# The slot table of the experts, built by matmuls of 0/1 rank tiles instead of a scatter through memory

## The reference, cut to what matters

```python
lg = (xf @ w_router_group + b_router_group)          # 4 groups
gi = argmax(lg); p_grp = max(softmax(lg))
le = (xf @ w_router_expert + b_router_expert).reshape(-1, 4, 8)
le_g = sum(le * one_hot(gi, 4)[:, :, None], axis=1)
top_v, top_i = top_k(le_g, 2)
wts = softmax(top_v) * p_grp                          # gate weights
e_idx = gi[:, None] * 8 + top_i                       # two of 32 experts a token
out = sum over the two: wts * (silu(x Wgate_e) * (x Wup_e)) Wdown_e
```

## Time and profile before

| what | us |
|---|---|
| median of 3 runs (1534.4 to 1539.6) | 1537.83 |
| the profiled execution | 1539.11 |
| its span, first to last instruction | 1537.4 |
| PE busy (81% of the span) | 1242.3 |
| DVE busy (34%) | 516.8 |
| POOL busy (18%) | 269.1 |
| ACT busy (13%) | 197.2 |

### The profile page before, as it was taken

The page is one execution under the profiler, slowest core; times in us unless marked ns, Lnnn a source line. Parts: engine busy times, 40 slices in busy tenths (PEclk is TensorE's granted clock), DMA queues, the critical chain, the costliest instruction groups (busy, mean ns, idle before and its releaser), DMA issues.

```text
span 1537.4 us, 14850 instructions
## 1 busy us (share of the span) xinstructions
PE 1242.3 (81%) x5948; PEld 683.2 (44%) x5948; DVE 516.8 (34%) x1014; ACT 197.2 (13%) x319; POOL 269.1 (18%) x580
## 2 busy tenths in 40 slices
PE   5899999998979797989979785877888786878625
PEld 2456556454546464656557472332333332333214
DVE  2412657544752862245531331211112111111044
ACT  1311111101201310231210220000000000000011
POOL 3170388870000000021120002010000010000010
PEclk9899999999998898889989866999899998899856
DMA  9998468765663636352122503999999999999441
GB/s 343 363 364 299 166 216 277 268 225 177 215 222 110 219 110 219 125 150 84 55 69 110 218 31 103 421 421 419 413 413 404 404 394 413 400 412 409 203 137 69
DMA packets 140342, 387.06 MB, mean 252 GB/s; under 512 B 15435, under 2 KB 54757, under 8 KB 112814
## 3 DMA queue, kind: packets, MB, share of 16 engines
q1 hardware_dynamic: 132208, 361.91, 62.4%
q0 software_dynamic: 6784, 18.76, 3.5%
q10 hardware_dynamic: 1280, 5.42, 1.0%
HBM read 385.97 MB, written 23.15 MB: 266 GB/s over the span
## 4 chain that ended last, share of the span: by engine, by line
PE 47%; DMA 26%; DVE 10%; POOL 10%; issue 3%; ACT 2%; SPq 1%; DVEq 0%; POOLq 0%; ACTq 0%
DMA slot<-in_w_exp_up 20%; PE psum L1402 10%; PE psum L1069 9%; PE psum L1102 5%; PE psum L1347 5%; PE psum L998 3%; PE psum L959 2%; DMA slot<-in_w_ada 2%; PE psum L968 2%; POOL mem L529 2%; POOL mem L532 2%; POOL sq L527 2%; POOL sq L530 2%; PE psum L1357 1%; POOL sq L528 1%
## 5 line engine op out<-in xcount | busy, mean ns | idle before, releaser
L1402 PE MATMUL psum<-slot,mem 128*64 128x512 f32 x1024 | 259.8, 667 | 83.6 <-DMA slot<-in_w_exp_up 82.7
L1069 PE MATMUL psum<-hT,slot 128*128 128x320 f32 (+1 forms) x1056 | 309.7, 454 | 19.8 <-DMA slot<-in_w_in 19.8
L1069 PEld LDWEIGHTS psum<-hT,slot 128*128 128x128 f32 (+1 forms) x1056 | 205.8, 198 | 120.5 <-issue 28.7
L1402 PEld LDWEIGHTS psum<-slot,mem 128*64 128x64 f32 x1024 | 86.0, 154 | 255.9 <-issue 170.8
L2110 DVE TENSOR_TENSOR sq<-sq,psum 128x256 f32<-128x256 f32 x16 | 6.8, 422 | 381.7 <-ACT sq L914 381.7
L1426 PE MATMUL psum<-mem,sq 128*64 128x512 f32 x512 | 113.4, 595 | 8.6 <-issue 7.1
L968 PE MATMUL psum<-slot,cT 128*8 128x512 f32 (+1 forms) x768 | 101.9, 639 | 16.9 <-DMA slot<-in_w_ada 16.9
L613 POOL DMA_INDIRECT moe_output<-mem,idx x16 | 15.9, 995 | 485.1 <-ACT mem L918 461.5
L1102 PE MATMUL psum<-mem,slot 128*128 128x320 f32 x256 | 78.5, 467 | 0.0
L1347 PE MATMUL psum<-mem,slot 128*128 128x320 f32 x256 | 72.2, 447 | 5.4 <-DVE mem L1945 5.4
L1426 PEld LDWEIGHTS psum<-mem,sq 128*64 128x64 f32 x512 | 42.0, 137 | 69.8 <-issue 67.9
(11 more groups left out here) (422 smaller groups left out, 1323.4 us busy)
## 6 DMA issues: line engine op xcount, KB each, us to landing
slot<-in_w_ada SPq DMA_DIRECT2D x48, 2048.0 KB, 13.7
slot<-in_w_exp_gate SPq DMA_DIRECT2D x64, 1024.0 KB, 13.4
slot<-in_w_exp_up SPq DMA_DIRECT2D x64, 1024.0 KB, 16.6
mem<-in_w_exp_down SPq DMA_DIRECT2D x32, 2048.0 KB, 18.2
slot<-in_w_in SPq DMA_DIRECT2D x17, 2048.0 KB, 17.3
slot<-in_w_out SPq DMA_DIRECT2D x8, 2048.0 KB, 9.0
mem<-in_w_in SPq DMA_DIRECT2D x2, 2048.0 KB, 17.9
mem<-in_x_prompt ACTq DMA_DIRECT2D x1, 2048.0 KB, 12.0
```

Source lines behind the costliest of these rows:

```text
L1069: last = mm(psum[0:wd, grp % 2, 0:T], w[:, k, q * P:q * P + wd], hT[:, k, :], start=(k == 0), stop=(k == KD - 1))
L1402: last = mm(psum[rows_, 0, :].rearrange("p (w n) -> p w n", w=2), xe[i % 2][:, k, rows_], gate_up[h][:, :, k, :], start=(k == 0), stop=(k ...
```

## The change

The table in memory, its six scatters and its read back go. In their place DVE builds, for each choice c and token tile j, a 0/1 tile `at_rank` (token by 64 ranks: 1 where the token's rank is that rank) and a tile `tok_of` (token by expert, holding the token number plus one where the token chose that expert, else 0; a second copy holds the row number plus one). The product, 64 ranks by 32 columns, summed over the six (c, j) in PSUM, is the slot table: 12 matmuls, six for even and six for odd experts, which land on partitions 0 to 63 and 64 to 127. DVE turns 0 into NOWHERE, subtracts one and casts into `slot_rows`, whose layout becomes two blocks of 16 columns. The numbers of `routed` move: 2 is `at_rank`, 3 is `slot_rows`, 4 the overflow counts, 5 `pos_gather`, 6 `spill`. The gate weights and what depends on them come behind the table. PE waits for `routed` 6 behind the first four `turn_x` instead of ahead of them. POOL's consts shrink from seven small steps to two.

```diff
 gpsimd:
-            pl(g.iota(eTi, pattern=[[1, NPAIR], [CAP * NPAIR, 2]], base=0, channel_multiplier=0))
-            for c in range(2):
-                pl(g.iota(tok_row[:, c, :, 0], pattern=[[P, 3]], base=0, channel_multiplier=1))
-                pl(g.iota(tok_row[:, c, :, 1], pattern=[[P, 3]], base=c * T, channel_multiplier=1))
-            pl(g.memset(slot_rows, NOWHERE), "slot_consts")
+            pl(g.iota(count_i, pattern=[[1, CAP]], base=0, channel_multiplier=0))
+            pl(g.iota(tok_next, pattern=[[P, 3]], base=1, channel_multiplier=1), "slot_consts")
-            pool.dma_start(tok_dram.rearrange("(p i) u -> p (i u)", p=P), slot_rows).then_inc(S("tokens_moved"), 16)
-            pool.wait_ge(S("tokens_moved"), 16)
...
             pool.wait_ge(S("routed"), 3)
-            for c in range(2):
-                for j in range(3):
-                    n = P if j < 2 else TS
-                    pool.indirect_dma_start(tok_dram, bass.IndirectOffsetOnAxis(ap=pos_scatter[0:n, 3 * c + j:3 * c + j + 1], axis=0),
-                                            tok_row[0:n, c, j, :], None, bounds_check=NE * CAP - 1, oob_is_err=False)\
-                        .then_inc(S("tokens_moved"), 16)
-            pool.wait_ge(S("tokens_moved"), 16 * 7)
-            pool.dma_start(slot_rows, tok_dram.rearrange("(p i) u -> p (i u)", p=P)).then_inc(S("tokens_moved"), 16)
-            pool.wait_ge(S("tokens_moved"), 16 * 8)
             pool.wait_ge(S("h2_stored"), 32)
 tensor:
             pe.wait_ge(S("routed"), 2)
+            for h in range(2):
+                for c in range(2):
+                    for j in range(3):
+                        n = P if j < 2 else TS
+                        last = mm(psum[CAP * h:CAP * h + CAP, 3, 128:160], at_rank[0:n, 3 * c + j, :],
+                                  tok_of[0:n, c, j, h].rearrange("p w i -> p (w i)"),
+                                  start=(c == 0 and j == 0), stop=(c == 1 and j == 2))
+            last.then_inc(S("rank"), 1)
+            pe.wait_ge(S("routed"), 4)
             mm(bank(3, 3), ones[:, :], rt[:, 496:499], start=True, stop=True).then_inc(S("rank"), 1)
...
             pe.wait_ge(S("act_rows"), 12)
-            pe.wait_ge(S("routed"), 5)
             for g_ in range(4):
                 turn_x(0, g_, 0)
+            pe.wait_ge(S("routed"), 6)
 vector, behind the one-hots (the same A1, A2 and Mk steps, now first; then):
+            st(v.memset(rk, 0.0))
+            dve.wait_ge(S("slot_consts"), 1)
+            st(v.tensor_copy(count_f, count_i))
+            st(v.tensor_copy(tok_f[:, 0, :], tok_next))
+            st(ts(tok_f[:, 1, :], tok_f[:, 0, :], float(T), None, ADD))
+            for c, A_ in enumerate((A1, A2)):
+                for w in range(2):
+                    st(tt(tok_of[:, c, :, :, w, :], A_.rearrange("p j (i h) -> p j h i", h=2),
+                          bc(tok_f[:, c * w, :].unsqueeze(2).unsqueeze(3), [P, 3, 2, NPAIR]), MUL))
+            dve.wait_ge(S("rank"), 1)
+            st(v.tensor_copy(rk[:, 0:2, :], bank(3, 64).rearrange("p (j e) -> p j e", j=2)))
+            st(v.tensor_copy(rk[0:64, 2, :], bank(3, NE, 64, lo=64)))
+            over, sl_, keep, at = rt[:, 484:490], rt[:, 490:496], rt[:, 500:506], rt[:, 472:478]
+            for c, A_ in enumerate((A1, A2)):
+                st(tt(am, A_, rk, MUL))
+                st(v.tensor_reduce(at[:, 3 * c:3 * c + 3].unsqueeze(2), am, AX.X, ADD))
+            st(tt(at_rank, bc(count_f.unsqueeze(1), [P, 6, CAP]), bc(at.unsqueeze(2), [P, 6, CAP]), ALU.is_equal), "routed")
+            st(ts(over, at, float(CAP), None, ALU.is_ge))
+            st(tt(rt[:, 496:499], over[:, 0:3], over[:, 3:6], ADD))
+            dve.wait_ge(S("rank"), 2)
+            found, row = psum[:, 3, 128:160], rt[:, 432:464]
+            st(ts(row, found, 0.0, float(NOWHERE + 1), ALU.is_equal, MUL))
+            st(tt(row, row, found, ADD))
+            st(ts(row, row, -1.0, None, ADD))
+            st(v.tensor_copy(slot_rows, row), "routed")
+            st(v.memset(rt[:, 471:472], 0.0), "routed")
+            st(ts(keep, over, -1.0, 1.0, MUL, ADD))
+            st(ts(sl_, tok_f.rearrange("p c j -> p (c j)"), -1.0, None, ADD))
+            st(tt(rt[:, 478:484], sl_, keep, MUL))
+            st(v.tensor_copy(pos_gather, rt[:, 478:484]), "routed")
+            dve.wait_ge(S("rt_exp"), 1)
   (here the six gate weight steps; then, as before, ge, A1 *= w1, A2 *= w2, comb (2), wk (2), rank, spill;)
-   (the old steps for eT, ge, Mk, over, pos_scatter, sl_ and pos_gather are gone from behind rank 1)
```

More of the change, by code:

```diff
@@ L262, in build @@
         U32 = mybir.dt.uint32
[L263 to L269, removed]
+        idx_ = sb("idx", [P, 44], U32)
+        pos_gather, spill, tok_next = idx_[:, 0:6], idx_[:, 6:7].bitcast(I32), idx_[:, 8:11].bitcast(I32)
+        slot_rows = idx_[:, 12:44]
         gate_up = [slot[:, 2 * h:2 * h + 2, :].rearrange("p w (k n) -> p w k n", k=KD) for h in range(2)]
@@ L281, in build @@
         tri = flat[:, 18432:18560]
-        eTi = flat[:, 18624:18656].bitcast(I32)
-        eT = tri[:, 0:32]
+        count_i = flat[:, 18592:18656].bitcast(I32)
         wr = flat[:, 18684:18684 + KD * 36].rearrange("p (k e) -> p k e", k=KD)
@@ L288, in build @@
         A1, A2, Mk, rk, ge, am = (sq[:, 0, 96 * i:96 * i + 96].rearrange("p (j e) -> p j e", j=3) for i in range(6))
+        at_rank = sq[:, 1, 0:384].rearrange("p (c r) -> p c r", c=6)
+        tok_of = rows[:, 0:384].rearrange("p (c j h w i) -> p c j h w i", c=2, j=3, h=2, w=2)
+        count_f, tok_f = rows[:, 384:448], rows[:, 448:454].rearrange("p (c j) -> p c j", c=2)
         sg = sq[:, 1, 0:256]
@@ L298, in build @@
         act_ = flat[:, 16320:16320 + 640]
-        tok_dram = nc.dram_tensor("rows_of_slot", [NE * CAP, 2], U32, kind="Internal").ap()
         h2_dram = nc.dram_tensor("moe_input", [T, D], F32, kind="Internal").ap()
@@ L444, in _ @@
             gate, up = (a[f"w_exp_{x}"][0].rearrange("e (k p) n -> e p k n", p=P) for x in ("gate", "up"))
-            sp.wait_ge(S("routed"), 5)
+            sp.wait_ge(S("routed"), 6)
             with sp.If(sp.value_load(spill[0:1, :], min_val=0, max_val=2 * T) > 0):
@@ L919, in _ @@
                  .then_inc(S("y_right"), 1)
-            act.wait_ge(S("routed"), 5)
+            act.wait_ge(S("routed"), 6)
             for j in range(3):
@@ L2043, in _ @@
             st(tt(rt[:, 240:243].unsqueeze(2), v2, v1, SUB), "rt_expo")
+            for g in range(4):
+                for A_, oh_ in ((A1, oh1), (A2, oh2)):
+                    st(tt(A_[:, :, 8 * g:8 * g + 8], oh_, bc(oh4[:, :, g:g + 1], [P, 3, 8]), MUL))
+            st(v.memset(A1[64:P, 2, :], 0.0))
+            st(v.memset(A2[64:P, 2, :], 0.0))
+            st(tt(Mk, A1, A2, ADD), "routed")
+            st(v.memset(rk, 0.0))
[28 more added lines that the diff above has]
+            st(v.tensor_copy(pos_gather, rt[:, 478:484]), "routed")
             dve.wait_ge(S("rt_exp"), 1)
@@ L2092, in _ @@
             st(tt(wk[:, 3:6].unsqueeze(2), w2, keep[:, 3:6].unsqueeze(2), MUL))
-            dve.wait_ge(S("rank"), 2)
+            dve.wait_ge(S("rank"), 3)
             st(v.tensor_reduce(rt[:, 499:500], bank(3, 3), AX.X, ADD))
```

32 lines of the change are left out of this document (2 added, 30 removed).

## The result

The changed kernel took 1526.87 us (median of 4, 1526.31 to 1531.13); the kernel before 1536.59 us (median of 4) beside it. The ratio is 0.994, 95% interval 0.9921 to 0.9959. Run twice more beside the kernel before, the same changed kernel gave 1529.96 us (6 executions; ratio 0.994, 0.9926 to 0.9955) and 1529.13 us (8 executions; 0.9949, 0.9932 to 0.9965). The forecast was 1530.0 us, 7.8 us faster, which is a ratio of 0.9949.

A forecast was written before the change was run, and what follows sets the result against it. The DMA stream of expert weights is full, but the router sets its start. Moving the first gather from 936.33 to 928.5 us, limited by the rows' store, saves 7.8 us: 1537.83 to 1530.0 us, range 1526.0 to 1535.0 us.

The forecast's parts named there:

- The gain is in the twelve microseconds between table and gather, and counts one to one: Between scatter positions and first gather, 12.43 us: gather at 928.5 instead of 936.33 us, 7.8 us gained, all on the path.
- Gate weights, earlier matrices and POOL's early part bring nothing: Ahead of the ranks: Mk some 1.8 us earlier, but rank matmuls queue behind transposes; PE does not wait for POOL.
- From the ranks to the table: DVE and PE from 919.1 us: copies, `at_rank`, twelve calls of 3.6 us, four DVE steps, to 926.0 us (925.1, 929.5).
- The store ends last: At POOL's first gather: store of rows lands at 927.7 us, gather at 928.5 us; the table alone would allow 926.9 us.
- the 0.8 us that the forecast left open: In the store of rows: without scatters beside it, it might land some 0.8 us earlier, giving 8.6 us instead of 7.8.
- Waits added: Behind the table: DVE's later steps end about 930.3 us, first gathered rows transposed from 933.1 us; at least 2.8 us left.
- The transposes in front of the ranks: PE before the ranks: they follow ACT's copies, which the change doesn't touch; end at 917.92 us, `rank` 1 stays at 919.1 us.
- The table as the later one: Rival at the first gather: table ends last, gather at 930.4 us, 5.9 us gained, 1531.9 us; chance 0.17.
- The clock that brings more: Rival at transposes and `hidden` 0: clock stays at 2.4 GHz, with faster store 11.1 us gained, 1526.7 us; chance 0.10.
- The stream that gives it back: Rival in the expert-weight stream: 1% less rate loses 4.7 us, leaving 3.1 us, 1534.7 us; no measurable change, chance 0.11.
- Slower by a late clock: Rival at `hidden` 0 and pair 0's down matmuls: 1.2 GHz all the way, 10.6 us lost, 1548.4 us; chance 0.05.

The follow-up runs named there:

- Twelve scatters: Kernel before with each of the six scatters sent a second time, into a second table nobody reads: 1545.27 us against 1537.89 us, ratio 1.005.
- the third profile: Profile from the third set of the changed kernel, no edit, beside the kernel before: 1529.13 us, ratio 0.9949.
- gate weights late: Kernel before with only the gate-weight steps moved behind `pos_gather`: ratio 0.9987 to the kernel before.
- Table twice: Changed kernel with the twelve matmuls of the table made twice: ratio 0.9976 to the kernel before.
- Fill: Changed kernel with 18 unread matmuls of 512 columns in PE's idle times at the router: ratio 0.9978 to the kernel before.
- both together: Changed kernel with the expert-input store in three parts from SP's queue and 15 unread 512-column matmuls in PE's idle times: 1531.08 us, ratio 0.9956.
- the pad: Changed kernel with 24 small unread matmuls far from the router, twelve behind each of pairs 5 and 9: 1531.5 us, ratio 0.9956.
- the store in three: Changed kernel with the expert-input store sent in three parts from SP's queue, each once its rows are copied: 1528.73 us, ratio 0.9946.
- wide logits: Changed kernel with router columns as weights and all 320 tokens moving, 16 logit calls for 48, then turned: 1519.8 us, ratio 0.9897.

## Why the prediction was right, point by point

- **The gain is in the twelve microseconds between table and gather, and counts one to one.** Right. Forecast 7.8 us; 7.8 us at the first load of pair 1 (72.61 to 64.81), 8.1 us between the means. Twelve scatters show the one to one from the other side. The time itself, 1526.87 us, was 3.1 us under the forecast, which is within the spread: the two later medians are 1529.96 and 1529.13 us.
- **Gate weights, earlier matrices and POOL's early part bring nothing.** Right; DVE's idle time in front of the ranks was 4.27 us after, with the `tok_of` steps already out of it, and the edit alone moved no scatter. Without POOL's store at 784 us PE waits 5.43 us for DVE ahead of its matmuls of 320 columns, as before.
- **From the ranks to the table.** Reckoned 6.9 us from 919.1 to 926.0 us; measured 6.92 us (920.17 to 927.09). `at_rank` 0.56 us as its row of before; the twelve calls 3.72 us where I took 3.6, in the third profile 2.80 us. That term came out by two errors that cancel. I let the clock fall at 922.9 us, in the middle of the calls; it fell at about 921.4 us (the granted clock is 1.00 from 921 to 921.4 us and 0.50 from 921.8 us on), so all twelve ran at the low level. And a call at the low level took 3.72 / 12 = 0.31 us, not 0.42 us. In the third profile the clock fell 1.6 us into the calls (1.00 to 928 us, 0.83 from 928 to 929 us, then 0.50). As the store ended last, none of this is in the gain.
- **The store ends last.** Right, and the size of the slack too: reckoned 928.5 - 926.9 = 1.6 us, measured 1.46 us, in the third profile 2.5 us. The last part of the store took 8.39 us against 8.5 us before, so the scatters had hardly slowed it, and the 0.8 us that the forecast left open for this did not come. The estimate from the Trainium skill (DMA: Bandwidth & Descriptors, Anatomy of one DMA) was 8.0 us from the first issue to landing; the trace has 928.55 - 919.73 = 8.82 us, so the row was the better guide, and the page's fit stands for another queue. That the fixed part is mostly the receipt of the last write no run here shows; the 1.90 us of the 16 KB read back bear out its size alone.
- **Waits added.** Right: `spill` was ready at 931.48 us, the first gathered rows were turned from 933.94 us. The margin was 2.5 us where I had 2.8.
- **What I had not in the sum.** The transposes in front of the ranks, which I had as untouched, took 6.25 instead of 5.35 us in the profiled execution. That made the gather only 53.91 - 46.86 = 7.05 us earlier there, and with equal transposes (third profile) 7.85 us. `hidden` 0, 0.68 us shorter, gave most of it back. Both are the clock: the granted clock was 0.68 on average over the transposes of before and 0.58 over those after, and 0.68 again in the third profile, where they took 5.36 us. Over `hidden` 0 it was 0.86 before and 0.90 after, and 1.00 where that took 13.95 us (gate weights late).
- **The rivals.** The table as the later one: not so, by 1.5 us. The clock that brings more: in part, as a `hidden` 0 of 15.50 instead of 16.2 us was named as its sign (the rival's 11.1 us left out the 1.5 us of the transposes that it names itself); `hidden` 0 took 13.95 us in one profile of the changed kernel, but also in one of the kernel before with the long idle time in front, so the shorter idle time isn't shown as the cause. The stream that gives it back: no. Slower by a late clock: 16.26 us was the longest `hidden` 0 in fourteen profiles.

What stays open: the kernels with matmuls added at the router that were slower than the changed one. Table twice has a mean of 1533.8 us in twelve executions against 1529.4 us, 4.4 us more; its one profile has the first load 1.0 us behind two profiles of the changed kernel (65.82 against 64.81 and 64.84) and 3.4 us behind the third (62.38). Fill has 4.2 us more, with 1.6 and 4.0 us; both together 1.6 us more, with a first load 1.0 us earlier. Table twice's profiled execution was 4.1 us longer than the changed kernel's first one: 5.0 us of that lie in front of the first logit matmul (887.62 against 882.62 us), 1.0 us between it and the first load, and the rest was 1.9 us shorter. With one profile of each, and the clock's level in another place each time, it can't be said how much of these 4 us is the router and how much the front, and the pad could not settle whether added instructions as such have a part in it.

## What to carry to other kernels

Ask of a chain that is to be cut which other wait stands beside its end, hidden under it: here a store of 8.4 us set the gain at 7.8 us, where the table alone allows 9.4 us (53.91 - 45.38 us with the store in three, and 0.9 us for the longer transposes). To move a small table between partitions, a product of 0/1 tiles with numbers took 2.8 to 3.7 us on PE, where six indirect DMAs, their landing and the read back took 10.7 us; with DVE's steps around it, from the ranks to a table that can be used, it was 6.9 against 16.4 us (919.11 to 935.51). In a stage where all other engines and the DMAs wait, look for its longest piece before the cleverest one: 48 thin matmuls at the low clock cost more than the whole table.

## What the runs showed of the hardware

The granted clock rose while PE did transposes only. In the third profile of the changed kernel (windows, columns as above), PE idles or transposes gathered rows up to 943.4 us, before any weight matmul:

```profile
934.00:939.00 5.00, 0.24 (x1) 0.27 (x2) 1.02 (x6) 0.00 (x0) 2.20 (x2) 0.50 0.40 108
939.00:943.40 4.40, 3.49 (x16) 2.83 (x15) 2.77 (x4) 0.00 (x0) 0.00 (x0) 0.62 0.12 47
```

The mean of 0.62 between 939 and 943.4 us means the full level for the last quarter of it (1.06 us), and `hidden` 0 then ran at 1.00 from its start. The Trainium skill (TensorE: Matmul & The Clock Gate, Part 4: PE-mode transpose) says that in one kernel the full clock didn't engage for matmuls in transpose mode. Here it did for the calls that the kernel makes as transposes, in f32; they leave one record each where its f32 matmuls leave two, which suggests that mode, but no row names it.

Indirect DMAs of 8 bytes a row cost POOL 1.22 to 1.42 us each from start to start (the scatters of four profiles; six from 924.77 to 931.28 us before), a gather of 8 KB a row 1.36 to 1.48 us, and POOL's wake-up ahead of the first one took 0.8 to 0.9 us. The 48 router matmuls of 36 columns ran for 21.8 us at 0.50 in all twelve profiles that have them; with the operands the other way round (wide logits) the mean was 0.50 from 883.2 to 886 us and 0.99 from 886 to 893.3 us.
